# First weight slot and first x pair fetched in halves, its split shared by three engines, and the first products taken two chunks at a time

## The reference, cut to what matters

```
h = rms_norm(x, norm1_w[l])
cols = split_cols(h @ w_in[l], IN_SIZES)
...
n_q, n_kc, n_vc, n_ks, n_vs, n_kw, n_vw, n_g = cols[3:11]
```

## Time and profile before

| | us |
|---|---|
| median of 3 runs (1790.41 to 1791.29) | 1790.88 |
| the profiled execution | 1791.22 |
| its span, first to last instruction | 1789.3 |
| TensorE busy | 1769.9 (99%) |
| GpSimd busy | 1096.6 (61%) |
| VectorE busy | 746.2 (42%) |
| ScalarE busy | 496.7 (28%) |

### The profile page before, as it was taken

One profiled execution on the slowest core, in us unless ns is written; L12 is line 12 of the kernel. 1 busy time (PEld: TensorE's weight loads), 2 busy tenths in 40 slices (PEclk: granted clock), 3 DMA queues, 4 the chain that ended last, 5 costly groups with the idle time before them and its releaser, 6 DMA issues.

```text
span 1789.3 us, 22449 instructions
## 1 busy us (share of the span) xinstructions
PE 1769.9 (99%) x8530; PEld 1422.0 (79%) x8530; DVE 746.2 (42%) x1267; ACT 496.7 (28%) x955; POOL 1096.6 (61%) x1149
## 2 busy tenths in 40 slices
PE   8999999999999999999999999999999999999998
PEld 5776767888888887778888888777888888888886
DVE  5438655230022235253006373545433587215532
ACT  3236663220021111322004232555300222222232
POOL 5643407777777787666776675554788574444442
PEclk9999999999999999999999999999999999999999
DMA  6620112223223223222322222222233223222331
GB/s 220 208 74 27 37 36 94 95 98 102 95 94 100 100 83 118 82 84 86 103 95 71 71 82 76 71 71 71 73 105 102 75 95 101 99 95 94 97 103 60
DMA packets 47054, 163.05 MB, mean 91 GB/s; under 512 B 5539, under 2 KB 6755, under 8 KB 46564
## 3 DMA queue, kind: packets, MB, share of 16 engines
q1 hardware_dynamic: 45740, 158.43, 26.5%
q10 hardware_dynamic: 1208, 3.19, 0.6%
HBM read 158.56 MB, written 2.12 MB: 90 GB/s over the span
## 4 chain that ended last, share of the span: by engine, by line
PE 94%; DVE 3%; ACT 2%; issue 1%; DMA 0%; POOL 0%; SPq 0%; DVEq 0%; ACTq 0%
PE bank L811 93%; DVE sq_sum L1822 1%; PE bank L1156 1%; PE bank L1202 1%; DMA w_raw<-in_w 0%; ACT sq L1412 0%; DVE tmp L1827 0%; ACT sb_e L1727 0%; DVE h_lo L1884 0%; ACT sb_e L1726 0%; POOL w_lo_t L2473 0%; DVE sq_parts L1854 0%; PE bank L1306 0%; DVE tmp L2189 0%; ACT att_l_t L1656 0%
## 5 line engine op out<-in xcount | busy, mean ns | idle before, releaser
L2473 POOL TENSOR_TENSOR w_lo_t<-w_raw,w_hi_t 128x256 fp32r<-128x256 f32 (+1 forms) x892 | 823.3, 952 | 167.9 <-ACT w_hi_t L1490 149.5
L2468 POOL TENSOR_SCALAR w_hi_t<-w_raw 128x1024 fp32r<-128x1024 f32 (+1 forms) x221 | 240.9, 1090 | 467.6 <-PE bank L811 431.1
L811 PE MATMUL bank<-h_hi,w_hi_t 128*128 128x512 f32 x1044 | 419.3, 402 | 8.5 <-POOL w_lo_t L2473 7.5
L811 PE MATMUL bank<-h_hi,w_lo_t 128*128 128x512 f32 x1044 | 407.5, 390 | 0.0
L811 PE MATMUL bank<-h_lo,w_hi_t 128*128 128x512 f32 x1044 | 401.5, 389 | 0.0
L811 PEld LDWEIGHTS bank<-h_hi,w_hi_t 128*128 128x128 f32 x1044 | 196.9, 189 | 61.0 <-issue 19.4
L811 PEld LDWEIGHTS bank<-h_hi,w_lo_t 128*128 128x128 f32 x1044 | 197.1, 189 | 41.1 <-issue 1.4
L811 PEld LDWEIGHTS bank<-h_lo,w_hi_t 128*128 128x128 f32 x1044 | 195.8, 188 | 42.7 <-issue 1.7
L811 PE MATMUL bank<-hid_hi,w_hi_t 128*128 128x512 f32 x432 | 168.0, 389 | 0.0
L811 PE MATMUL bank<-hid_lo,w_hi_t 128*128 128x512 f32 x432 | 168.0, 389 | 0.0
L811 PE MATMUL bank<-hid_hi,w_lo_t 128*128 128x512 f32 x432 | 168.0, 389 | 0.0
(11 more groups left out here) (360 smaller groups left out, 2486.4 us busy)
## 6 DMA issues: line engine op xcount, KB each, us to landing
w_raw<-in_w SPq DMA_DIRECT2D x276, 512.0 KB, 3.2
y<-in_w SPq DMA_DIRECT2D x6, 512.0 KB, 6.0
x_sb<-in_x SPq DMA_DIRECT2D x4, 512.0 KB, 7.6
x_sb<-in_x ACTq DMA_DIRECT2D x2, 1024.0 KB, 5.2
out_y<-x_sb SPq DMA_DIRECT2D x8, 256.0 KB, 2.4
u_raw<-in_w SPq DMA_DIRECT2D x2, 512.0 KB, 6.4
toep<-table SPq DMA_DIRECT2D x4, 256.0 KB
decay<-in_decay SPq DMA_DIRECT2D x1, 1024.0 KB, 4.7
```

Source lines behind the costliest of these rows:

```text
L811: return pe.matmul(out, lhs, rhs, start=start, stop=stop, **kw)
L2468: pool.tensor_scalar(hi[:, 0:cols], raw[:, 0:cols], 1.0, 0.0, ALU.mult, ALU.add).then_inc(*did("w_hi", i))
L2473: ins = pool.tensor_tensor(lo[:, piece], raw[:, piece], hi.bitcast(F32)[:, piece], ALU.subtract)
```

## The change

Five edits, all for the first 26 us.

1. SyncE fetches slot 0 in two halves of 512 columns (own semaphore `w_half` for the first), and x chunks 0 and 1 singly (`x_head` and `x_in0`). The order of the queue is now: half of slot 0, chunk 0, the other half, chunk 1, x pair 1, slot 1, x pairs 2 and 3, slot 2.
2. ScalarE and VectorE split the first half of slot 0 (chunks 0 to 3), GpSimd the second (chunks 4 to 7).
3. TensorE starts kvc when VectorE's half is split, and waits for GpSimd's half at chunk 4.
4. kvc's chunks 0 and 1 are taken with high and then low products, then chunks 2 and 3 so, then chunks 4 and 5 with all three products each.
5. ksw's chunks 0 to 5 follow with all three products each; chunks 6 and 7 of both stay as they were.

```diff
-    run([("fmk", ("kvc",), "h", 0, 4, "hi"), ("fmk", ("ksw",), "h", 0, 4, "hi"),
-         ("fmk", ("kvc", "ksw"), "h", 0, 4, "lo"), part(4, KD)])
+    for k in (0, 2):
+        run([("fmk", ("kvc",), "h", k, k + 2, "hi"), ("fmk", ("kvc",), "h", k, k + 2, "lo")])
+    run([("fmk", ("kvc",), "h", 4, 6), ("fmk", ("ksw",), "h", 0, 6), part(6, KD)])
...
-        "n1": ([x_sb[:, c] for c in range(KD)], P, T, ones, 1 / D, "eps", [("x", c // 2) for c in range(KD)]),
+        "n1": ([x_sb[:, c] for c in range(KD)], P, T, ones, 1 / D, "eps", [("x", c // 2 if c else "head") for c in range(KD)]),
...
-            pe.wait_ge(*after("w_lo", i))
-            if i == SPLIT[0]:
-                pe.wait_ge(*after("first_lo"))
+            pe.wait_ge(*(after("first_lo") if i == SPLIT[0] else after("w_lo", i)))
...
+                if SLOTS[names[0]][0] == SPLIT[0] and k0 == 4:
+                    pe.wait_ge(*after("w_lo", SPLIT[0]))
...
-        act.wait_ge(C.sem["w_landed0"], 16)
-        act.activation(w_hi[0][:, 512:1024], w_raw[:, 0, 512:1024], ACT.Copy).then_inc(*did("first_hi"))
+        act.wait_ge(C.sem["w_half"], 16)
+        act.activation(w_hi[0][:, 0:512], w_raw[:, 0, 0:512], ACT.Copy).then_inc(*did("first_hi"))
...
-        dve.tensor_tensor(w_lo[0][:, 512:1024], w_raw[:, 0, 512:1024], w_hi[0].bitcast(F32)[:, 512:1024],
+        dve.tensor_tensor(w_lo[0][:, 0:512], w_raw[:, 0, 0:512], w_hi[0].bitcast(F32)[:, 0:512],
...
-                cols = 512 if n == 0 else 1024
-                pool.tensor_scalar(hi[:, 0:cols], raw[:, 0:cols], 1.0, 0.0, ALU.mult, ALU.add).then_inc(*did("w_hi", i))
+                mine = slice(512 if n == 0 else 0, 1024)
+                pool.tensor_scalar(hi[:, mine], raw[:, mine], 1.0, 0.0, ALU.mult, ALU.add).then_inc(*did("w_hi", i))
...
-        for g in range(4):
-            if g < FIRST_LOADS:
-                sp.dma_start(w_raw[:, g], a["w"][g]).then_inc(C.sem[f"w_landed{g}"], 16)
+        sp.dma_start(w_raw[:, 0, 0:512], a["w"][0][:, 0:512]).then_inc(C.sem["w_half"], 16)
+        sp.dma_start(x_sb[:, 0], a["x"][:, 0]).then_inc(C.sem["x_head"], 16)
+        sp.dma_start(w_raw[:, 0, 512:1024], a["w"][0][:, 512:1024]).then_inc(C.sem["w_landed0"], 16)
+        sp.dma_start(x_sb[:, 1], a["x"][:, 1]).then_inc(C.sem["x_in0"], 16)
+        sp.dma_start(x_sb[:, 2:4], a["x"][:, 2:4]).then_inc(C.sem["x_in1"], 16)
+        sp.dma_start(w_raw[:, 1], a["w"][1]).then_inc(C.sem["w_landed1"], 16)
+        for g in (2, 3):
             sp.dma_start(x_sb[:, 2 * g:2 * g + 2], a["x"][:, 2 * g:2 * g + 2]).then_inc(C.sem[f"x_in{g}"], 16)
```

More of the change, by code:

```diff
@@ L372 @@
 U_WEIGHT = {"n1": "norm1", "n2": "norm2", "pre_u": "pre", "fpre": "fpre"}
-SEMAPHORES = """x_in0 x_in1 x_in2 x_in3 x_back ones_set r_cols mask_in mixer_in kv_in ksw_in kr_in kr_turn kr_again mla_w zeros table_out sq_pe const_in wqb_in misc_in late_in alibi_in alibi_s bias_in y_out
+SEMAPHORES = """w_half x_head x_in0 x_in1 x_in2 x_in3 x_back ones_set r_cols mask_in mixer_in kv_in ksw_in kr_in kr_turn kr_again mla_w zeros table_out sq_pe const_in wqb_in misc_in late_in alibi_in alibi_s bias_in y_out
 w_hi wa_hi w_lo slot_used v_chain s_chain sq_s sq_v rstd rstd_used ms_lo
@@ L708, in wait_src @@
         else:
-            eng.wait_ge(C.sem[f"x_in{w[1]}"], 16)
+            eng.wait_ge(C.sem["x_head" if w[1] == "head" else f"x_in{w[1]}"], 16)
     def att(u):
@@ L2466, in _ @@
             else:
-                cols = 512 if n == 0 else 1024
-                pool.tensor_scalar(hi[:, 0:cols], raw[:, 0:cols], 1.0, 0.0, ALU.mult, ALU.add).then_inc(*did("w_hi", i))
+                mine = slice(512 if n == 0 else 0, 1024)
+                pool.tensor_scalar(hi[:, mine], raw[:, mine], 1.0, 0.0, ALU.mult, ALU.add).then_inc(*did("w_hi", i))
                 pool.wait_ge(*after("w_hi", i))
             size = 256 if n == 0 or i in IN_PIECES else 1024
-            for k in range(0, cols if n == 0 else 1024, size):
+            for k in range(512 if n == 0 else 0, 1024, size):
                 piece = slice(k, k + size)
```

## The result

The kernel after takes 1796.58 us (median of 8 runs, 1795.43 to 1797.56), the kernel before, beside it, 1791.41 (8 runs, 1790.41 to 1793.11): ratio 1.0028, 95% interval 1.0020 to 1.0037. That is 5.2 us slower, within the range and 1.4 us above the forecast; 0.5 of the 1.4 is the kernel before, 1791.41 here against the 1790.88 that the forecast started from. The profiled execution took 1796.56, against 1791.22 before: +5.34, which the first 30 us have to explain.

What follows compares the result with a forecast made beforehand. TensorE's single matmul stream bounds the kernel (busy 1769.9 of 1789.3 us). Product order +2.9 and slow clock +1.4 make +4.3: 1795.5 profiled, 1795.2 us predicted as median (55%; own range 1794.2 to 1797.0), whole range 1791.6 to 1797.2.

Steps and rivals of the forecast that it cites:

- The start: TensorE's first product at 5.7 instead of 7.5 us, 1.8 earlier, but this gain cannot come through to the end.
- The landings: Slot 1 lands fourth, at 9.6 instead of 8.16; short rows add 0.25 us, with 0 and 0.6 as ends.
- The turns: VectorE and GpSimd exclude each other by whole instructions; each VectorE turn costs GpSimd 0.55 us; low part 5 ready at 18.8.
- The order: Low product of chunk 5 stands ahead of all ksw matmuls; 37 matmuls from 18.8 end at 27.2 against 24.28: +2.9 us.
- The clock: After TensorE's stop of nearly 4 us, matmuls go slow: +1.4 us, half of the start's 2.8.
- At nothing: Priced at zero: two more DMA issues, SyncE's next loads about 1.4 us later, and the squares' adds.
- The squares' adds: VectorE's adds end again at about 24 us, hidden since TensorE asks for the sum at 27.2; no cost.
- Slot 3's later load: SyncE's next loads wait for slot 1's split, about 1.4 us later; used only after these matmuls, so no cost.
- The clock held: Rival, 23%: low part 5 as forecast but no slow matmuls behind TensorE's stop: +2.9 us, 1793.8.
- The low part did not get in early: Rival, 15%: low part 5 precedes slot 2's subtract, ready about 16.3; +0.4 to +1.8 us, about 1792.
- the two engines do not exclude each other: Rival, 7%: VectorE and GpSimd run freely, low part 5 at about 13.3, the early start comes through: 1789.1 us.
- Of the halves, the first landed sooner: Rival that slot 0's halves land no sooner: TensorE starts at 7.5, result as forecast; no price of its own.

Runs made afterwards that it cites:

- the two repeats: Kernel after, unchanged, profiled two more times: 1796.71 and 1796.86 us.
- the run with whole transfers: Kernel before, all transfers whole, only slot 1's load moved one place back, behind x pair 1: 1793.0 us, ratio 1.0011.
- pieces: Kernel after, with GpSimd's subtracts of slots 1 and 2 cut into four of 256 columns: 1793.16 us, ratio 1.0006 to before.
- held-back subtract: Kernel after, with GpSimd's subtract of slot 2 waiting for low part 5 and cut in four: 1794.28 us, ratio 1.0013 to before.
- the run with the stop filled: Kernel after, with 14 unused matmuls ahead of the low product of chunk 5, where TensorE idled: 1795.47 us, ratio 1.0019 to before.
- the order alone: Kernel before with only the new list of products, old loads and split of slot 0: 1795.15 us, ratio 1.0019.
- the two repairs together: Kernel after, kvc's low products 4 and 5 behind ksw's chunks 0 to 3, slot 2's subtract awaiting low 5, cut in four: 1795.2 us, ratio 1.0020 to before.
- the low products later: Kernel after, with low products of kvc's chunks 4 and 5 moved behind ksw's chunks 0 to 3: 1792.14 us, ratio 1.0005 to before.

## Why the prediction was right, and what was off

**The start.** First product at 5.59, forecast 5.7. Right, and worth as little as said: the 1.9 us were spent again by 14.65.

**The landings.** Slot 1's conversion began at 10.10, forecast 9.6: 0.77 behind the 9.33 of its new place where I took 0.25 and kept 0.6 as the end; 10.43 and 10.25 in the two repeats, and 9.88 to 11.06 over the nine executions with the new loads, eight of them beyond that end of 9.93. (In the prediction's sum for the 0.25, 2.75 and 2.49 us are already the times of 1.05 MB; the factor 1.05 stands there once too often and changes little.) Chunk 1 had to wait for the first half of a slot, a chunk and the other half, with itself 1.05 MB in short rows, in the slowest part of the start. Windows of before and, below, of after, in the same columns:

```profile
4.00:6.00 2.00, 0.00 (x0) 0.00 (x0) 0.53 (x1) 0.63 (x1) 1.05 (x2) 1.00 0.93 252
6.00:8.00 2.00, 0.47 (x1) 0.50 (x2) 0.72 (x2) 1.33 (x2) 1.43 (x2) 1.00 1.02 404
8.00:10.00 2.00, 1.57 (x4) 0.66 (x2) 0.85 (x2) 0.67 (x2) 1.76 (x2) 1.00 1.03 420
```

```profile
4.00:6.00 2.00, 0.41 (x1) 0.45 (x2) 1.13 (x2) 1.26 (x2) 0.00 (x0) 1.00 0.86 260
6.00:8.00 2.00, 0.78 (x2) 0.06 (x1) 0.31 (x1) 0.48 (x1) 1.00 (x2) 1.00 0.96 345
8.00:10.00 2.00, 1.70 (x4) 1.20 (x5) 1.61 (x2) 1.45 (x3) 1.03 (x2) 1.00 1.01 385
```

From 6 to 10 the rate was 59 and 35 GB/s lower, 2 x 59 + 2 x 35 = 188 KB in all, or 0.45 us at 420. This difference in rate comes with the halves and not with the execution: from 6 to 8 the nine executions with halves moved 314 to 362 GB/s and the five with whole transfers 393 to 408, from 8 to 10 372 to 410 against 416 to 426. The halves have shorter rows and are smaller transfers; which of the two slows them was not separated. How much of the 0.77 is theirs stays open too, as slot 1's conversion began at 9.92 in the run with whole transfers.

**The turns.** Low part 5 was ready at 18.80, as forecast to the hundredth, but by two errors that cancel. GpSimd's four instructions took 1.18 + 2.69 + 1.49 + 2.66 = 8.02 instead of 6.96, so VectorE's three turns cost it 1.06 in all, 0.35 each and not 0.55; that gave back the half microsecond by which the slot was late. The mechanism is shown: pieces bring the low part to 15.79, a held-back subtract to 16.58.

**The order.** 37 matmuls at the fast spacing are 8.4 us, and 18.86 + 8.4 = 27.26; the forecast had 27.2, the run with the stop filled 27.20. Right.

**The clock: the term that was mis-sized.** I took half of what the start costs, seven slow matmuls and 1.4 us, between 0 and 2.8. In the profile twelve intervals took 24.05 - 18.86 = 5.19 us instead of 12 x 0.227 = 2.72: 2.47 us. By the same working the repeats cost 1.92 and 2.63. About 0.1 of each is not the clock: the first interval behind such a stop takes 0.33 at the fast spacing too (18.09 to 18.42 in the order alone). The excess, 2.47 - 1.4 = 1.1, is what the sum lacked: 4.3 forecast, 5.46 at sq_sum. In two of the three executions the full 2.8 was nearer than half of it. The Trainium skill ("TensorE: Matmul & The Clock Gate", What's actually happening) says that the count of slow matmuls at a kernel's start is "run-variable"; the trace agrees and shows it behind a later stop, with none and eight behind the same stop of 3.2 us in one program.

**At nothing.** The squares' adds ended at 21.25 + 2.27 = 23.52, six microseconds ahead of their reader. Slot 3's later load was not missed: behind 30 us TensorE waits no longer than before. Both right here, but the adds' cover was thin, as the two repairs together showed.

**The rivals.** The clock held in one execution of the order alone and in one with the stop filled; in the kernel after it held in none of three. The low part did not get in early by itself; where the pieces or the held-back subtract bring it early, the medians are 1793.2 and 1794.3 and not about 1792. That the two engines do not exclude each other is ruled out by the pieces. Of the halves, the first landed sooner and the second later.

**What stays open.** Why the clock falls behind two stops of 1.48 and 1.14 us in one kernel, holds behind one of 3.20 in another, and falls at 36 us in a third with no stop near it; and what divides the runs of the kernel before into 1790.4 to 1791.7 and 1792.2 to 1794.0. No version beat the kernel before; the nearest are those with pieces and with the low products later, whose intervals hold 1.

## What to carry to other kernels

Before moving a product forward in an engine's queue, ask when the slowest of its inputs is ready, and lay the engines that share a resource side by side to see who ends when the other does. A fast engine's stop is priced by what follows it as well as by its length: take the slow stretch at its full size, and as something that may differ between executions. An earlier first instruction is worth nothing if the second input pays for it with its place in the queue.

## What the runs showed of the hardware that I had not expected

- The granted clock can fall after TensorE has already resumed: in the second execution of the order alone four matmuls went at the fast spacing and then eight slow (19.37 to 22.74; the clock was 1.00 from 17 to 19 and 0.64 from 19 to 20). It can also fall far from any long stop: 0.51 from 38 to 40 us in one execution and from 236 to 238 in another, 1.5 and 1.6 us each.
- Two executions of one program differ by 1.87 us of 1795, 0.20 by a later stop and the rest by the clock, so part of what looks like noise at this size has a place in the timeline.
- The first transfers ran at 252 and 260 GB/s from 4 to 6 us in the two kernels; from 8 to 10 they were at 420 with whole transfers and 385 with halves. The second 512 KB were there between 6.60 and 6.80 with the old loads and between 7.09 and 8.48 in halves.
- A turn that VectorE takes cost GpSimd 0.35 us in the kernel after (mean of three), less than the 0.53 to 0.56 by which VectorE ends behind it.
